# GpSimd makes the sums of three of the six later modulation weights

## The reference, cut to what matters

```
mod_x = silu(c) @ w_mod + b_mod          # 1024 -> 6 x 1024: sh1x, sc1x, g1x, sh2x, sc2x, g2x
hx  = rmsnorm(x) * (1 + sc1x) + sh1x     # before attention; the same with c_ctx for the context rows
x   = x + g1x * attention(hx, context)   # 16 head units here, each with two score matrices
hx2 = rmsnorm(x) * (1 + sc2x) + sh2x
x   = x + g2x * peer(hx2)                # gathers 16 expert rows for each row and head, 8 heads
```

## Time and profile before

| | us |
|---|---|
| median of 3 runs | 1495.84 (1495.03 to 1495.87) |
| the profiled execution | 1496.79 |
| its span in the profile | 1494.7 |
| PE busy | 1333.3 (89%) |
| DVE busy | 1073.7 (72%) |
| ACT busy | 603.2 (40%) |
| POOL busy | 273.4 (18%) |
| DMA | 416.18 MB, mean 278 GB/s |

### The profile page before, as it was taken

How to read it: one execution, slowest core, us unless ns; L and a number is a source line. 1 busy time by engine, 2 the same in 40 slices (tenths; PEclk the granted TensorE clock), 3 DMA queues, 4 the chain that set the end, 5 groups by cost and what they waited for, 6 DMA issues and landing times.

```text
span 1494.7 us, 18510 instructions
## 1 busy us (share of the span) xinstructions
PE 1333.3 (89%) x6164; PEld 915.2 (61%) x6164; DVE 1073.7 (72%) x2251; ACT 603.2 (40%) x1228; POOL 273.4 (18%) x263
## 2 busy tenths in 40 slices
PE   7998999988797979798897798989999999899998
PEld 2786664534343434353343346669999876799987
DVE  4598857776767677676777757877887477788864
ACT  5333643212122222213132215565665455656652
POOL 0000004544333344444434220000000000000000
PEclk9999999999898989999899899999999999999999
DMA  9623536999999999999999996433544433344540
GB/s 396 252 113 132 207 137 254 421 421 421 422 422 422 422 422 422 422 422 422 421 421 422 420 385 255 166 116 135 201 173 177 163 140 142 114 169 182 204 151 28
DMA packets 49845, 416.18 MB, mean 278 GB/s; under 512 B 5488, under 2 KB 5616, under 8 KB 7024
## 3 DMA queue, kind: packets, MB, share of 16 engines
q0 software_dynamic: 36864, 268.45, 43.2%
q1 hardware_dynamic: 12912, 146.82, 25.7%
HBM read 414.20 MB, written 1.05 MB: 278 GB/s over the span
## 4 chain that ended last, share of the span: by engine, by line
PE 52%; DMA 16%; DVE 14%; issue 9%; POOL 5%; ACT 3%; POOLq 0%; DVEq 0%; ACTq 0%; SPq 0%
DMA ring<-in_uv,ids 14%; PE ps L1091 6%; PE ps L1345 6%; PE ps L1346 6%; PE ps L1347 6%; PE ps L1159 4%; PE ps L1161 4%; PE ps L1160 4%; POOL arena L733 3%; POOL ring L733 3%; DVE arena L2053 2%; PE ps L938 2%; PE ps L868 2%; PE ps L869 2%; PE ps L870 2%
## 5 line engine op out<-in xcount | busy, mean ns | idle before, releaser
L1091 PE MATMUL ps<-arena 128*128 128x512 f32 x512 | 256.8, 658 | 93.9 <-ACT arena L1559 93.7
L1091 PEld LDWEIGHTS ps<-arena 128*128 128x128 f32 x512 | 106.1, 211 | 237.5 <-issue 126.7
L1091 PE MATMUL ps<-ring,arena 128*128 128x512 f32 x512 | 227.0, 596 | 3.7 <-ACT arena L1559 3.7
L564 DVE TENSOR_TENSOR arena_r<-ring,arena_r 128x1024 fp32r<-128x1024 f32 x152 | 184.9, 1223 | 58.0 <-ACT arena_r L549 57.6
L733 POOL DMA_INDIRECT arena<-in_uv,ids x128 | 135.7, 1060 | 496.9 <-issue 258.6
L2053 DVE CUSTOM_DVE_ANT_0 ring<-ring,arena 128x1024 f32<-128x1024 f32 x128 | 153.2, 1223 | 72.7 <-DMA ring<-in_uv,ids 72.6
L1345 PE MATMUL ps<-hH,arena_r 128*128 128x256 f32 x704 | 199.4, 283 | 0.0
L1347 PE MATMUL ps<-hH,arena_r 128*128 128x256 f32 x704 | 199.2, 283 | 0.0
L1346 PE MATMUL ps<-arena_r 128*128 128x256 f32 x704 | 199.2, 283 | 0.0
L2053 DVE CUSTOM_DVE_ANT_0 arena<-arena 128x1024 f32<-128x1024 f32 x128 | 153.1, 1223 | 60.4 <-DMA arena<-in_uv,ids 59.9
L549 ACT ACTIVATE arena_r<-ring 128x1024 fp32r<-128x1024 f32 x152 | 158.9, 1053 | 58.9 <-PE ps L1161 58.6
(11 more groups left out here) (315 smaller groups left out, 1992.3 us busy)
## 6 DMA issues: line engine op xcount, KB each, us to landing
ring<-in_lw SPq DMA_DIRECT2D x39, 2048.0 KB, 7.7
ring<-in_b1w SPq DMA_DIRECT2D x18, 2048.0 KB, 8.9
wqb<-in_wq SPq DMA_DIRECT2D x8, 1024.0 KB, 9.0
ring<-in_lw SPq DMA_DIRECT2D x8, 1024.0 KB, 5.1
ring<-in_lw SPq DMA_DIRECT2D x2, 1088.0 KB, 11.5
arena<-in_uv,ids POOLq DMA_INDIRECT x128, 20.0
ring<-in_uv,ids POOLq DMA_INDIRECT x128, 23.4
cst<-in_const SPq DMA_DIRECT2D x1, 1487.5 KB, 18.7
```

The costliest lines, as they stand in the source:

```text
L564: nc.vector.tensor_tensor(low_of(l, p), piece_raw(p), high_of(l, p).bitcast(F32), ALU.subtract)\
L1091: last = nc.tensor.matmul(ps[:, 4 + 2 * c + b, :], diag[:, k % 4, :], vrows[at[k]][:, b * 512:(b + 1) * 512], start=False, stop=(close and ...
```

## The change

VectorE makes the parts of weights 0, 1 and 2 only (24 parts: 21 before attention as before, then two in unit 0 and one in unit 1). Weights 3, 4 and 5 go to GpSimd, which scales the eight parts in their slot, in place, and adds them up as a tree: four 512-wide parts to four, two to two, and the last pair into `macc`. Its instructions stand ahead of its wait for the first ids, in the order: products of 3, products of 4, total of 3, products of 5, total of 4, total of 5. TensorE's `mod_total` and SyncE's release of slots 12 to 14 wait for GpSimd's totals.

```diff
-MODB_PARTS = (2, 2, 2, 2, 2, 2, 2, 2, 3, 3, 3, 2, 0, 0, 0, 0)
+MODB_PARTS = (2, 1) + (0,) * 14
+MODB_POOL = 3
+POOL_STEPS = KD + 2
...
+        pool_sum, pool_total = sem("pool_sum"), sem("pool_total")
...
+        def mod_products(pool, i):
+
+            n = MODB_SLOT[i]
+            wait_slot(pool, n)
+            at = POOL_STEPS * (i - MODB_POOL)
+            for k in range(KD):
+                nc.gpsimd.tensor_scalar(slot(n)[:, k, :], slot(n)[:, k, :], sil2[:, k, 0:1], None, ALU.mult)\
+                    .then_inc(pool_sum, 1)
+            pool.wait_ge(pool_sum, at + KD)
+            nc.gpsimd.tensor_tensor(slot(n)[:, 0:4, :], slot(n)[:, 0:4, :], slot(n)[:, 4:8, :], ALU.add)\
+                .then_inc(pool_sum, 1)
+            pool.wait_ge(pool_sum, at + KD + 1)
+            nc.gpsimd.tensor_tensor(slot(n)[:, 0:2, :], slot(n)[:, 0:2, :], slot(n)[:, 2:4, :], ALU.add)\
+                .then_inc(pool_sum, 1)
+            pool.wait_ge(pool_sum, at + KD + 2)
+
+        def mod_last(pool, i):
+
+            n = MODB_SLOT[i]
+            pool.wait_ge(modcol_done, MOD_A + i - 1)
+            nc.gpsimd.tensor_tensor(macc[:, i % 2, :], slot(n)[:, 0, :], slot(n)[:, 1, :], ALU.add)\
+                .then_inc(pool_total, 1)
...
-                    sp.wait_ge(mod_sum, KD * (MODB_SLOT.index(n) + 1))
+                    i = MODB_SLOT.index(n)
+                    if i < MODB_POOL:
+                        sp.wait_ge(mod_sum, KD * (i + 1))
+                    else:
+                        sp.wait_ge(pool_total, i - MODB_POOL + 1)
...
+            mod_products(pool, 3)
+            mod_products(pool, 4)
+            mod_last(pool, 3)
+            mod_products(pool, 5)
+            mod_last(pool, 4)
+            mod_last(pool, 5)
             pool.wait_ge(first_ids, 1)
...
-                pe.wait_ge(mod_sum, KD * (i + 1))
+                if i < MODB_POOL:
+                    pe.wait_ge(mod_sum, KD * (i + 1))
+                else:
+                    pe.wait_ge(pool_total, i - MODB_POOL + 1)
```

More of the change, by code:

```diff
@@ L1937, in _ @@
                     heads_variance(0)
-            assert part_at == KD * MOD_B
+            assert part_at == KD * MODB_POOL
             def square_of_chunk1():
```

## The result

| | before | changed |
|---|---|---|
| median, us | 1495.86 (4 runs) | 1514.03 (1512.15 to 1515.38, 4 runs) |
| ratio | | 1.012, 95% interval 1.0106 to 1.0133 |
| span of the profiled execution | 1494.7 | 1511.2 |
| mean granted clock | 0.958 | 0.949 |

The change costs 18 us. The forecast was +4.8, with a range up to 1508.5: the sign was right, the size was not. All of it arises in attention: the first gather starts 16.28 us later (252.59 against 236.31 in the earlier trace rows) and the span ends 16.5 later, so the one-to-one step held.

The account below looks back on a forecast made before the run. PE was taken to lead the first block's attention stage, in short turns with ACT and DVE. Terms: -2.3 us relief + 7.1 contention = +4.8, so 1500.6 us against the median; range 1492.5 to 1508.5.

Parts of the forecast that it names:

- the one-to-one step: A shift of the first block's attention stage should reach the end of the kernel one to one, through the first gather.
- (d): PE's granted clock dips differently in attention as matmuls spread otherwise: 1 to 2 us either way, part of every case.
- GpSimd's price: Per weight on GpSimd: scalings 0.70 us each, additions 4.08, 2.09 and 1.09; weight 4 ready at 174.9, 2.5 us to spare.
- The relief, 2.3 us: Removed VectorE products shorten three PE waits in attention by 0.5, 1.24 and 0.53 us, sum 2.3.
- The start at 134 us: GpSimd can start on weight 3 at 134 us, slots issued at 126.14 and the quickest load taking 7.8.
- the slots: SyncE's slots 16 to 18, released by GpSimd's totals, still load in time: worth nothing either way.
- the one-to-one passage: The attention stage's shift passes in full to the first gather and the kernel's end.
- a scaling moves each element in and out: Bounds for a 128x512 GpSimd scaling, priced from memsets: 0.50 us if the two overlap, 0.90 if not.
- rival (b): GpSimd's totals come late to PE in attention without any contention: about 1498 to 1507; chance 0.17.
- The meetings, 7 x 1.02 = 7.1 us: From 134 to 178 us, seven VectorE operations each wait 1.02 us for GpSimd's current instruction: 7.1 us.
- the seven large operations: VectorE's 4 probability operations and 3 kept products of weight 2, from 134 to 178 us, expected to wait for GpSimd.
- rival (c): VectorE's small attention instructions wait for GpSimd too, 10 to 12 more waits: +12 us, about 1508; chance 0.15.

Follow-up runs that it names:

- e1: The changed kernel without GpSimd's part, sums of weights 3 to 5 left out; 1493.87 us, ratio 0.9986 against the kernel before.
- e6: The changed kernel with 36 short memsets a weight instead of GpSimd's scalings and additions, totals about as late; 1516.53 us, ratio 1.0146.
- e2: The changed kernel with memsets of about the same lengths in place of GpSimd's scalings and additions; 1518.17 us, ratio 1.0149.
- e7: The kernel of e4 with only weight 5 on GpSimd and weights 0 to 4 on VectorE; 1504.98 us, ratio 1.0061.
- e8: e1 with two 128x3072 reductions on VectorE ahead of unit 2's probabilities, GpSimd idle; 1505.18 us, ratio 1.0065.
- e4: The changed kernel with GpSimd's additions cut into pieces of 128x512; 1516.54 us, ratio 1.0145.
- e9: e1 with scalings by immediate, scalings by column, copies and broadcast products on GpSimd, on idle buffers; 1494.26 us in a single run.
- e3: The kernel before, all products on VectorE, with GpSimd doing the same scalings and additions on idle buffers; 1523.83 us, ratio 1.0192.
- e10: The kernel before, nothing on GpSimd, with VectorE's 27 parts spread otherwise over the units; 1493.56 us, ratio 0.9982.
- e5: e1 with GpSimd's scalings and additions on idle buffers, no total waiting for them; 1510.84 us, ratio 1.0102.

## Why the prediction was wrong, point by point

The sum was -2.3 + 7.1. The step that failed is that nothing stood in it for PE's clock, which (d) put at 1 to 2 us either way: behind its stalls PE worked at half clock, for 10.9 of the 16.3 us of the stage. The other two terms came out at -1.1 and +7.0, the second by luck, since other instructions were held than those that it counted. GpSimd's price was a second step that failed: because of it a second loss of about the same size lay under the first.

- **The relief, 2.3 us:** right in size (e1: 2.2), in part by luck. PE's three waits fell by 1.45 us, because at two of them ScalarE ended next, which the prediction had left out where it took the whole 1.24 and 0.53. The rest of e1's gain isn't explained; its short stretch at half clock (139 to 142.5 us) lies in another place than that of before, so the two traces don't compare to the tenth.
- **The start at 134 us, the slots, the one-to-one passage:** right (134.09; nobody waits for a slot; 16.28 at the gather, 16.5 at the end).
- **GpSimd's price:** the additions were in their bounds (4.5, 2.34, 1.26 us against 3.28 to 4.87, 1.69 to 2.48, 0.90 to 1.29), the scaling was not: 1.56 against 0.50 to 0.90. The second step that failed is "a scaling moves each element in and out": an upper end made from memory traffic did bound a copy (0.61), but not this operation; what makes it cost 1.56 us stays open. Weight 4 came at 195.9, not 174.9. At that price rival (b) was due, and e6 shows it alone (+20.8).
- **The meetings, 7 x 1.02 = 7.1 us:** the mechanism was right for GpSimd's additions only, and the count was wrong. Behind an addition the hold is the rest of it, as assumed (ends at 151.52 and 151.50). Beside a scaling, which lasts 1.6 us, it was 0.43 us at most; the prediction had taken the two as one kind. Of the seven large operations the three kept products met scalings alone and were not held (746 ns); the small ones, set aside as rival (c), carried most: 6.7 us on the negated maximum and 5.2 on L1934, of 14.5. The argument against (c), that one of them has two elements and one input, was wrong: size is no protection, and e2 shows that one input is none. That 7.0 us of added stalls are close to 7.1 is luck: they are one stall of 6.62 and one of 1.79. The Trainium skill, "SBUF — State Buffer", section "Who interferes with whom", has both forms: two SBUF inputs against GpSimd's reads (e2, where GpSimd only writes, agrees with 752 ns), and `tensor_scalar` in a two-port mode against any GpSimd instruction, the second engine blocking for the whole instruction (L1924 at 681 ns and e2's 906 agree, at two elements; that it ran in such a mode no run shows). The prediction had weighed only the first. Beside GpSimd's scalings, which read too, the measurements agree with neither form: 0.43 us at most in the changed kernel, and 0.3 on two products in e7.
- **The clock:** half clock for 21.9 us, and e8 shows that a stall of 6.7 us costs 11.3. The rows of before had it in small (0.90 from 160 to 170 us in the earlier trace rows, half clock from 160 to 162), and the prediction expected such dips to move, not to grow behind a stall.
- **Two limits, one visible:** the test named for (b), L799 starting as the total ends, was nearly met (196.14 against 195.9), with no idle time in front. Without e4 and e6 one would have called lateness harmless.

## What to carry to other kernels

Before work is moved to an idle engine, take the gain from the idle pieces of the engine that leads, not from the busy time that is moved: here 17 us of VectorE were worth 2, and a better spread of the same parts got them without the move. Where two engines hold each other, they do so at small instructions too, so count instructions, not elements; and ask which of the other's instructions hold and how long each lasts. Here it was the additions, up to 4.5 us, and hardly the scalings. Short additions alone didn't help (e4), since the scalings, 38 of GpSimd's 62 us, still made it late. If PE may stall for some microseconds, price its clock too; and where two limits lie close together, test each alone before calling one of them harmless.

## What the runs showed of the hardware that had not been expected

- On GpSimd a 128x512 fp32 `tensor_scalar` took 1.56 us with an immediate or a column factor, a copy 0.61, a product with the factor broadcast as a tensor 1.13, an addition 1.26 (e9 and the changed kernel).
- A two-element VectorE `tensor_scalar` was held 0.5 us on average and 2.6 at most by GpSimd's arithmetic in the changed kernel (3.5 at most in e3), and 0.7 on average by memsets (e2); a one-element product with two tensor inputs was held up to 4.0 us by an addition and not at all by memsets (e2: 0.22 us at each).
- It was the additions that held, not the scalings: beside GpSimd's `tensor_scalar` the longest hold in the changed kernel was 0.43 us, though they were 38 of its 62 us.
- After 6.6 to 7.2 us without matmuls PE worked 11 us at 1.2 GHz (the changed kernel, e8). Shorter idle times stood before a fall too: 1.79 us in the changed kernel (10.4 us at half clock behind it) and 2.50 us in e7 (3.51 us for 16 matmuls that otherwise take 1.90). Behind the 2.2 to 2.7 us of idle time at about 137, which every variant has, it fell to half in some executions (the changed kernel, e1, e7, e10) and not in others (before, e5). What decides that was not tried.
